# Where a later tile's row maxima stand among the attention's matmuls

## The reference, cut to what matters

```
# latent attention: 4 heads, 1024 queries, causal
s = einsum('bqhd,bkhd->bhqk', q, k);  s = where(kpos <= qpos, s, -1e30)
p = softmax(s);  out = einsum('bhqk,bkhd->bqhd', p, v)
# sparse attention, for each block of 128 queries: three branches, each
s_b = q . k_b - slope_h * distance, masked;  o_b = softmax(s_b) @ v_b
#   b=0: 63 compressed keys   b=1: all blocks up to the query's   b=2: the last 512 keys
out = g0 * o_0 + g1 * o_1 + g2 * o_2
```

## Time and profile before

| | |
|---|---|
| median of 3 runs | 3052.94 us (3047.82 to 3062.91) |
| profiled execution | 3055.21 us, span 3053.4 us |
| PE busy | 2911.6 us (95% of the span) |
| DVE busy | 1542.1 us (51%) |
| ACT busy | 805.1 us (26%) |
| mean granted TensorE clock | 0.973 of full |
| attention's steps | about 450 to 712 us in the first layer, about 1955 to 2218 us in the second |

### The profile page before, as it was taken

The page is one execution under the profiler, slowest core; times in us unless marked ns, Lnnn a source line. Parts: engine busy times, 40 slices in busy tenths (PEclk is TensorE's granted clock), DMA queues, the critical chain, the costliest instruction groups (busy, mean ns, idle before and its releaser), DMA issues. The chain is left out here.

```text
span 3053.4 us, 37080 instructions
## 1 busy us (share of the span) xinstructions
PE 2911.6 (95%) x14754; PEld 2341.3 (77%) x14754; DVE 1542.1 (51%) x2567; ACT 805.1 (26%) x1311; POOL 291.8 (10%) x242
## 2 busy tenths in 40 slices
PE   5999979999999999999989998899999999999997
PEld 5899856656788888888778997565577888888885
DVE  5645443554544444444655554616465444444457
ACT  3322123434221112112223222234432121112121
POOL 3212122000000000000221211210000000000003
PEclk9999979999999999999999999899999999999998
DMA  4113242103021111111121233330030111011111
GB/s 165 61 56 95 90 102 56 28 1 127 17 77 43 41 55 56 43 41 56 56 80 41 72 114 92 73 70 1 1 138 29 55 55 56 30 53 56 56 42 55
DMA packets 145778, 185.94 MB, mean 61 GB/s; under 512 B 33200, under 2 KB 119856, under 8 KB 145608
## 3 DMA queue, kind: packets, MB, share of 16 engines
q1 hardware_dynamic: 145608, 183.57, 19.3%
HBM read 153.83 MB, written 29.72 MB: 60 GB/s over the span
## 5 line engine op out<-in xcount | busy, mean ns | idle before, releaser
L950 DVE TENSOR_TENSOR h<-h,dense_acc 128x512 f32<-128x512 f32 x448 | 301.7, 685 | 202.8 <-PE dense_acc L778 202.8
L456 PE MATMUL dense_tr<-x_hi,mlp_w1hi 128*128 128x512 f32 x1024 | 400.3, 391 | 3.8 <-PEq L543 3.8
L776 PE MATMUL dense_acc<-mlp_w2hi,mlp_ahi 128*128 128x512 f32 x1024 | 399.2, 390 | 4.2 <-DVE mlp_alo L941 4.2
L458 PE MATMUL dense_tr<-x_hi,mlp_w1lo 128*128 128x512 f32 x1024 | 399.8, 390 | 0.0
L457 PE MATMUL dense_tr<-x_lo,mlp_w1hi 128*128 128x512 f32 x1024 | 399.7, 390 | 0.0
L778 PE MATMUL dense_acc<-mlp_w2hi,mlp_alo 128*128 128x512 f32 x1024 | 399.1, 390 | 0.0
L777 PE MATMUL dense_acc<-mlp_w2lo,mlp_ahi 128*128 128x512 f32 x1024 | 399.1, 390 | 0.0
L935 DVE TENSOR_TENSOR mlp_square<-mlp_square 128x512 f32<-128x512 f32 x128 | 88.3, 691 | 440.3 <-ACT mlp_square L857 440.3
L776 PEld LDWEIGHTS dense_acc<-mlp_w2hi,mlp_ahi 128*128 128x128 f32 x1024 | 192.6, 188 | 45.3 <-issue 5.4
L456 PEld LDWEIGHTS dense_tr<-x_hi,mlp_w1hi 128*128 128x128 f32 x1024 | 193.2, 189 | 44.3 <-issue 4.2
L458 PEld LDWEIGHTS dense_tr<-x_hi,mlp_w1lo 128*128 128x128 f32 x1024 | 192.9, 188 | 40.2
(11 more groups left out here) (316 smaller groups left out, 5338.3 us busy)
## 6 DMA issues: line engine op xcount, KB each, us to landing
ahead<-w_mlp SPq DMA_DIRECT2D x32, 1024.0 KB
mlp_raw<-w_mlp SPq DMA_DIRECT2D x32, 1024.0 KB, 4.8
ahead<-w_in SPq DMA_DIRECT2D x20, 1024.0 KB, 6.5
residual<-h SPq DMA_DIRECT2D x16, 512.0 KB, 2.6
projections<-h SPq DMA_DIRECT2D x16, 512.0 KB, 4.2
mix_qkvg<-projections SPq DMA_DIRECT2D x16, 512.0 KB, 4.7
h<-residual SPq DMA_DIRECT2D x16, 512.0 KB, 4.5
projections_T<-h SPq DMA_DIRECT2D x14, 512.0 KB, 3.4
```

What stands on the lines that cost most here:

```text
L456: pe.matmul(tr[:, n, :], wh, xh, start=(k == 0), stop=False)
L458: mm = pe.matmul(tr[:, n, :], wl, xh, start=False, stop=(k == KT - 1))
L776: pe.matmul(out[:, m % 4, :], xh, wh, start=(begin and j == 0), stop=False)
L950: dve.tensor_tensor(part, part, out[:, m % 4, :], ALU.add).then_inc(s.down_added, 1)
```

## The change

Outside steps 15 to 42 the pieces of the maxima (item 6) move in PE's loop from the end of the step to between `score_T(n)` (item 2) and `values(n - 1)` (item 3). In steps 15 to 42 the order stays, and but for the compression nothing stands there (no pieces are planned for them). No instruction is added or removed, and the loops of DVE, ACT, POOL and SP stay as they are.

```
                         score_T(n)
-                        if n:
-                            values(n - 1)
+                        if CMP0 <= n < MAX0:
+                            if n:
+                                values(n - 1)
+                        else:
+                            maxima(behind[n])
+                            if n:
+                                values(n - 1)
...
-                        maxima(behind[n])
+                        if CMP0 <= n < MAX0:
+                            maxima(behind[n])
```

## The result

| | before | after |
|---|---|---|
| median of 4 runs | 3057.93 us (3047.82 to 3063.88) | 3110.09 us (3099.24 to 3117.04) |
| ratio to before, 95% interval | | 1.0172 [1.0143, 1.0201] |
| profiled execution | 3055.21 us | 3113.99 us |
| mean granted clock in it | 0.973 | 0.962 |

The change makes the kernel slower by 52 us. The sign and the place were forecast; the size (3087 us, range 3070 to 3102) was not.

A forecast was written before the change was run, and what follows sets the result against it. PE, busy for 95% of the span, bounds the kernel. Twelve stalls, 16.2 us per layer, plus 0.5 for steps 0 to 12 give 16.7, 33.4 for two layers: 3088.6 on the profiled 3055.2, 3086.3 by the median, stated as 3087, range 3070 to 3102.

The forecast's parts named there:

- the mechanism: DVE may reduce a step's pieces only after writing the turned sum, which PE turns later; PE waits at twelve places.
- The steps with one piece and one piece: Steps 57, 58, 61, 65, 73, 74, 84, 96, 97: the piece reaches back over a further step; nothing counted.
- rival (A): The clock falls too, step 56 deciding: up to 5 us more per layer, so 3097 us; chance 0.12.
- step 56's stall: Steps 56 to 57, a query step: PE arrives at 1.38, the reduction needs 4.49; stall 3.1 us, net 2.8.
- 33.4: Twelve places at 16.2 us per layer plus 0.5 for steps 0 to 12: 16.7 per layer, 33.4 for two.
- steps 0 to 12: Both engines nearly full; early start in step 1 against losses in steps 5 and 9: +0.5 us per layer.
- the stalls behind steps 5 and 9: DVE waits longer for the turned sum, by a pair of pieces, and loses about 1 us each.
- the earlier start in step 1: Pieces run before the first values' product, so DVE starts about one product earlier; wins 1 us in the lower bound.
- +49: Upper bound of the sum in us, if the top of steps 0 to 12 holds and the clock falls.
- (B): Not slower: DVE keeps up, the twelve places cost nothing; 3047.6 us, by the median 3045 to 3053; chance 0.06.
- (C): Only the four query chains bite, DVE's write elsewhere starting sooner than read: +15 us, so 3068; chance 0.05.
- (D): The later values' product covers ACT's exponential: 3055 us on the profiled execution, 3053 by the median; chance 0.01.

The follow-up runs named there:

- the filled kernel: New order in steps 49 to 57 alone, plus unread matmuls on PE ahead of the waiting pieces: 3074.48 us, ratio 1.0059 to the kernel before.
- the pair of runs with steps 49 to 57 alone: New order in steps 49 to 57 alone, against the kernel before: 3097.95 us, 1.0113; the same with unread matmuls ahead of waiting pieces: 3074.48 us, 1.0059.
- the first experiment: Changed kernel with DVE's reductions moved ahead of the write and query_lows: 3057.09 us, ratio 0.9977 to the kernel before.

## Why the prediction was wrong

**Right: what bounds it, and the mechanism.** PE's waits for sparse reductions were to rise from 2.0 to 25 to 35 us: 26.4. PE's product was to wait for nothing in the sparse steps: so it is. With DVE's order turned round, the waits are gone. One sign failed: PE's busy time was to stay unchanged and grew by 29.6 us, which points at the clock.

**Right: the places, and nearly their sizes.** Layer 1, read against forecast:

| piece of step | forecast wait | measured |
|---|---|---|
| 50 | 0.9 | 0.44 |
| 51 | 2.3 | 2.21 |
| 52 | 1.5 | 1.35 |
| 53 | 1.6 | none |
| 54 | 0.9 | 0.27 |
| 56 | 2.1 | 0.49 + 1.25 |
| 57 | 3.1 | 2.67 |
| 65 / 70 / 80 / 86 / 92 | 1.7 / 1.3 / 0.8 / 0.8 / 0.8 | 1.47 / 1.16 / 0.66 / 0.64 / 0.67 |

Each is smaller than forecast, most of them by a little; one more, of 0.83 us behind step 104, was not foreseen. The steps with one piece and one piece do not stall, as argued. At step 53, and for a part of the way to step 54, PE itself was at half speed, and so came late enough to wait little or not at all: part of a stall was paid as slow matmuls. For step 53 a run bears this out: with the queries alone ahead of the reductions and the clock still full, that piece waited 1.33 us. Without the low clock the stalls of these steps come to 10.4 us, by the filled kernel; I had 10.8. From 58 on the idle time is 5.4 more, as forecast, but with the unforeseen 0.83 in it.

**The step that failed: the clock was left out of the sum.** I held it as rival (A) with a chance of 0.12, priced it at "up to 5 more per layer", let it hang on step 56's stall and dismissed it with "nearly as long isn't as long". What the runs showed in its place: the clock fell before that stall was reached, at 600 us behind 2.21 and 1.35, and once more around 1.25 and 2.67, 17 us of low clock per layer; with waits of 1.5 us at most it fell still.

The price is 5 to 8 us per layer: 8 (4 to 12) by the ratios of the pair of runs with steps 49 to 57 alone, 5.5 and 6.6 by their windows, 4.6 and 5.0 by the windows of the whole change (37.42 less 32.42 the latter). With the forecast's 33.4 it gives 43 to 49 in all. By its own text the forecast was wrong "if the clock in these windows is below 1.00"; it was 0.78 and 0.77.

The Trainium skill, "TensorE: Matmul & The Clock Gate", section "A second HAM failure mode: psum-queue depth-cycling", has a kernel in which TensorE idles briefly between groups of matmuls so often that its clock swings between the two levels. The trace at 594 to 606 us agrees with that section, and I had weighed the one before it, on single long gaps.

The row that spoke against (A), clock 1.00 with waits of up to 0.62 us in the same steps, was of the first layer alone, and of waits a quarter as long. In the second layer of the same profile the same waits stand beside a clock of 0.93 (24.54 us from 2075.12), so even that row was no safe ground.

**A second step, mis-sized: steps 0 to 12.** +0.5 per layer, from bounds of -1 and +3. Alone they cost 2.9 per layer (interval 0.6 to 5). PE's waits for the latent reductions rise to 4.6 us over both layers (1.2 before, as in the kernel with DVE's reductions first), and idle time by 1.6 per layer: the stalls behind steps 5 and 9 came, and a gain from the earlier start in step 1 shows nowhere. (The forecast called itself wrong if the first steps lost more than 3 us; over both layers they did.) The rest is likely clock, but low clock in these steps differs by several us between the layers of one run, and between kernels that have the old order there. All the kept profiles together bear the size out: from the first scores to those of step 15 a layer takes 31.6 to 34.1 us with the old order, 34.9 to 37.2 with the new one, and 32.4 to 34.8 with the new one and DVE's reductions ahead of its write.

**The range** ended at 3102: its upper bound, +49, from the median shown then. The change costs 52, and in the runs taken beside it the kernel before has a median of 3057.93, which is 5 us more. Of the 8 us that are missing, 5 are such scatter of the base and 3 are the sum. What was measured part by part, 35 + 6 + 9 = 49, is as much as that bound: what had been set as the edge was the likely case, and the range had nothing above it.

**The other rivals.** (B), not slower: it needed DVE to keep up, and it did only once DVE's own order was changed; then the result was 0.9977, on the side (B) had named. (C), only the query chains: refuted, the write alone costs +5.2 in steps 49 to 58, and the steps from 58 on have no query chain and lose 4.9. (D): the cover was worth nothing, as the unchanged 6.2 us show.

## What to carry to other kernels

When work is moved ahead on the engine that produces, read the queue of the engine that consumes: a result that is ready earlier is worth nothing if the consumer has an instruction ahead of it that waits for what the producer now does later. Move the consumer's order with it. And once the sum holds several stalls of 1 to 3 us close together on TensorE, put the clock into the likeliest case, not into a rival.

## What had not been expected of the hardware

- The clock fell in a stretch without any wait above 1.5 us (0.88 over 28.27 us), not only behind a 3.2 us one. Single short falls came with still less: in the second layer of the kernel before, with waits of 0.38 and 0.62 us (0.93 over 24.54 us), and in the first layer of the filled kernel, with 0.56 us at most (0.95 over 33.57 us). So these runs give no length of wait below which the clock is safe.
- 83 unread matmuls per layer, in time in which PE would have idled, made the kernel 0.54% faster (1.0113 to 1.0059, the intervals leave 0.3 to 0.8%).
- Matmuls in the new order run a little denser where nobody waits in either kernel. The kernel with DVE's reductions first, then the one before, from the scores of step 92 to those of step 105, 105 matmuls in each:

```profile
674.21:698.95 24.74, 24.74 (x109) 14.49 (x107) 13.23 (x28) 9.32 (x16) 0.00 (x0) 1.00 0.00 1
```

```profile
659.49:684.66 25.17, 25.17 (x107) 14.50 (x107) 12.96 (x28) 9.54 (x16) 0.00 (x0) 1.00 0.00 1
```

That is 1.7% of these steps. From the scores of step 50 to those of the last step the two kernels take 136.80 and 139.10 us, with about the same idle time (1.08 and 1.15); twice that difference is 4.6 us, the size of the first experiment's gain (4.9 by the medians), so it is likely its source. Why it is so stays open. So does what decides the length of a fall, which was 17 us in the whole change and 20 in the part of it.
